# Expert weights in a two-layer transformer kernel: three chunks of each next expert go through spare memory and a GpSimd copy

## The chip, the cores and the metric

The kernel runs on one core of one Trainium2 chip, as one launch. The metric is the device time of one execution in microseconds (us): the median of several runs. Lower is better.

## What is computed

The reference is a first block (modulated attention, then a mixture of experts) followed by a second one of two layers (retention with sparse attention, then a gated recurrence, each with a dense feed-forward part), all in float32 on 256 tokens of width 1024. The part around the change is the mixture of experts of the first block:

```
N_EXPERTS = 32; TOP_K = 4; D_FF_EXPERT = D_MODEL = 1024
...
h2 = rms_norm(x, g_pre_ffn[l]) * (1.0 + sc2) + sh2
f = moe_ffn(h2, w_router[l], b_router[l], w1[l], b1[l], w2[l], b2[l])
x = x + gt2 * rms_norm(f, g_post_ffn[l])
```

Each token goes to four of 32 experts. An expert is a 1024x2048 matrix w1 with a bias b1, a clipped gated activation, and a 1024x1024 matrix w2 with a bias b2; that is 12 MiB of float32 weights. The 32 experts together are 384 MiB, and every one is read in full from device memory.

## The kernel before, in words

All weights of the program pass through one **ring** of twelve places in SBUF (`ring0` to `ring11`), each of 128 partitions x 2048 float32, 1 MiB. A place holds one **chunk**. Chunk n goes to place n % 12. SyncE (SP) issues all weight transfers, in one fixed order, in the function `_(sp)` from line 476 on; before each it waits until the place's last reader on TensorE has finished. TensorE tells that with the semaphore `chunk_done`, and within the experts with `job_chunk`, raised once by every chunk read. A transfer that has landed raises `landed[place]` by 16, and TensorE waits for that before it reads (line 984, `chunk_here`).

**Experts.** An expert has twelve chunks: 0 to 7 are the eight row blocks of w1 (line 530), 8 to 11 the four double row blocks of w2. TensorE works in **jobs** of 64 token slots (`SLOTS`). A job (`expert`, line 1025) runs `first_matrix` (line 987: eight chunks, eight matmuls of 512 columns each), the bias (line 996), the scatter of the job before (line 974), the gather of tokens for a later job (line 958), the turn of the activations (line 1003), and `second_matrix` (line 1015: four chunks, eight matmuls each). An expert with more than 64 tokens has two jobs in a row, which read the same twelve chunks; for the last job of expert e the vector engine has put the count of chunks before it into the table `jobs`, and it tells with `ends_listed` that it has. There are 34 jobs for these inputs, so two experts have a second job.

SP's loop `expert_chunks` (lines 522 to 532) issues the twelve chunks of expert e + 1 in order, chunk j after `job_chunk >= last_job + j + 1`, that is, when the last job of expert e has read its chunk j. Expert 0's chunks come into the places that the projections of the first block leave.

**The activation.** In a job, VectorE clips the two halves (lines 2344 and 2345), multiplies them (line 2348), and multiplies by ScalarE's sigmoid (line 2350); then TensorE may turn the result (line 1003).

**GpSimd (POOL)** does little: it issues small transfers, among them the table `late` of 3516 columns (1.8 MB: decay, cosines, sines, masks of the second block) when the heads of the first attention are done (`mix_saved`, lines 597 and 598), and the 1 MiB `cmp_w1` after `ssq_ready` 2, that is after the experts (line 602). It also adds squares (line 609) and multiplies one block by the last gain (line 619, which raises `y_gained`). TensorE waits for `late_loaded` ahead of the second block's projections (line 1292), and VectorE waits for it at line 2407.

**Memory used before the experts and not in them:** the attention bias `alibi` in `early_sb`, and in the arena `nat_bias` and the attention scores (columns 6144 to 12288). `late_sb` lay at columns 9600 and up.

```
def expert_chunks(e, wait):
    for j in range(PER_EXPERT):
        wait(j)
...
expert_chunks(0, lambda j: slot_free(C_MOE + j))
sp.wait_ge(S.ends_listed, 1)
with sp.Fori(0, E_N - 1) as e:
    last_job = sp.value_load(...)
    expert_chunks(e + 1, lambda j: sp.wait_ge(S.job_chunk, last_job + (j + 1)))
```

Of the kernel before, what the change touches and what calls it, by code (L numbers as in the profile page):

```python
# [10 lines left out]
ALU = mybir.AluOpType  # L11
# [13 lines left out]
DIFF_HEADS = 4  # L25
UNITS = 8
# [7 lines left out]
E_N = 32  # L34
# [4 lines left out]
LISTED = 64  # L39
# [15 lines left out]
RING = 12  # L55
CHUNK = 2048
N_ADA_A, N_WIN, N_ADA_B, N_WOUT = 8, 12, 16, 4
PER_EXPERT = 12
FIRST_HOME = (6, 7, 0, 3)
C_ADA_A = 0  # L60
C_WIN = C_ADA_A + N_ADA_A
# [2 lines left out]
C_MOE = C_WOUT + N_WOUT  # L64
# [44 lines left out]
ADDED_NORMS = (2,)  # L109
# [149 lines left out]
cmp_pos cmp_hidden cmp_bias cmp_act cmp_out cmp_saved cmp_scores cmp_shift cmp_exp cmp_probs cmp_turned cmp_turn_saved  # L259
nsa_max nsa_probs nsa_weighted nsa_out nsa_closed  # L260
hg_level hg_scores hg_placed hg_out hg_saved hg_sq hg_ssq hg_root hg_gated
ffn_split ffn_part ffn_kept ffn_sum ffn_silu ffn_hidden y_gained y_total y_root y_scale y_out_saved y_out_also out_stored""".split()


class Chain:
# [14 lines left out]
def two_layer_program(nc, x, c, w_ada, b_ada, g_pre_mix, g_post_mix, w_in, w_out, lam_q1, lam_k1, lam_q2,  # L280
# [4 lines left out]
    with ExitStack() as ctx:  # L285
        def sbuf(name, cols, dt=F32, rows=P):
            return ctx.enter_context(nc.sbuf_tensor(name, [rows, cols], dt))

        S = namedtuple("Semaphores", NAMES)(*[ctx.enter_context(nc.semaphore(n)) for n in NAMES])
        landed = [ctx.enter_context(nc.semaphore(f"landed{i}")) for i in range(RING)]  # L290


        ring = [sbuf(f"ring{i}", CHUNK) for i in range(RING)]
# [3 lines left out]
        mixT = sbuf("mixT", KT * T)  # L297
# [3 lines left out]
        jobs = sbuf("jobs", 2 * LISTED + 2 + E_N, I32, rows=1)  # L301
# [10 lines left out]
        def const(name):  # L312
            return early_sb[:, EARLY[name][0]:EARLY[name][1]]

        ident, ones, before, slot_id, fold, window = (
            const(n) for n in ("ident", "ones", "before", "slot", "fold", "window"))
        eps6, eps5 = const("eps")[:, 0:1], const("eps")[:, 1:2]
        alibi = const("alibi").rearrange("p (h n) -> p h n", h=DIFF_HEADS)
        cols_a, cols_b = carve(P), carve(2)

        silu_c = carve(KT * 32).rearrange("p (k m) -> p k m", m=32)
# [13 lines left out]
        def region(at, cols):  # L335
            assert at + cols <= 15900
            return arena[:, at:at + cols]
# [52 lines left out]
        diag = sq[:, 1024:1280]  # L390
        wanted, rank_of, chosen, job_scratch = (region(8512 + ALL_JOBS * i, ALL_JOBS) for i in range(4))
        job_cols = region(9580, 4)

        late_sb = region(9600, N_LATE)
        assert 9600 + N_LATE <= 13312 + 256
# [63 lines left out]
        final_gain, sum_slots = hT[:, 0:1024], cmp_act  # L459
        y_sums, y_total, y_mean = sum_slots[:, 0:5], sum_slots[:, 8:10], sum_slots[:, 10:11]  # L460
        junk = [region(1536, 512), region(2048, 512)]

        def x_block(a, half):
            return x_rows[:, a, 512 * half:512 * half + 512]
# [13 lines left out]
        def _(sp):  # L478
            def slot_free(n):

                if n >= RING:
                    sp.wait_ge(S.chunk_done, n - RING + 1)

# [37 lines left out]
            w1_view = w1[0].rearrange("e (k p) n -> e k p n", p=P)  # L521
            w2_view = w2[0].rearrange("e (c p k) n -> e c p k n", p=P, k=2)

            def expert_chunks(e, wait):
                for j in range(PER_EXPERT):
                    wait(j)
                    home = ring[(C_MOE + j) % RING]
                    if j < 8:
                        src = w1_view[bass.ds(e, 1), j].rearrange("a p n -> p (a n)")
                    else:  # L530
                        src = w2_view[bass.ds(e, 1), j - 8].rearrange("a p k n -> p (a k n)")
                    sp.dma_start(home[:, :], src).then_inc(landed[(C_MOE + j) % RING], 16)  # L532

            expert_chunks(0, lambda j: slot_free(C_MOE + j))
            sp.wait_ge(S.ends_listed, 1)
            with sp.Fori(0, E_N - 1) as e:
                last_job = sp.value_load(jobs[0:1, bass.ds(e + (2 * LISTED + 2), 1)], min_val=0, max_val=PER_EXPERT * 48)
                expert_chunks(e + 1, lambda j: sp.wait_ge(S.job_chunk, last_job + (j + 1)))

            sp.wait_ge(S.count_ready, 1)  # L540
            last_job = sp.value_load(jobs[0:1, 2 * LISTED + 1:2 * LISTED + 2], min_val=0, max_val=PER_EXPERT * 48)
# [30 lines left out]
        def _(pool):  # L572
# [21 lines left out]

            pool.wait_ge(S.mix_saved, DIFF_HEADS)
            pool.dma_start(h_tok, x[0].rearrange("(a p) d -> p a d", p=P)).then_inc(S.tok_loaded, 16)
            pool.wait_ge(S.mix_saved, UNITS)
            pool.dma_start(late_sb, late).then_inc(S.late_loaded, 16)

            pool.wait_ge(S.ssq_ready, 2)  # L600
            for i, v in enumerate((cmp_w1_k_2, cmp_w1_v_2)):
                pool.dma_start(cmp_w1_sb[:, i, :, :], v[0].rearrange("(j p) n -> p j n", p=P)).then_inc(S.cmp_loaded, 16)

# [12 lines left out]
            pool.dma_start(final_gain, bass.AP(final_norm_g_2.tensor, 0, [[0, P], [1, D]])).then_inc(S.late_loaded, 16)  # L616
            pool.wait_ge(S.late_loaded, 32)
            pool.wait_ge(S.sq_ready, down_squares_at(1, 3))
            nc.gpsimd.tensor_tensor(x_block(0, 0), x_block(0, 0), final_gain[:, 0:512], ALU.mult).then_inc(S.y_gained, 1)

        N_VEC = 9 + 4

# [2 lines left out]
        def _(pe):  # L625
# [663 lines left out]
                    pe.wait_ge(S.turned_saved, UNITS + (RET_SSQ_AT[p] - NSA_FIRST) // NSA_STEP)  # L1289
                nc.tensor.matmul(bank[RET_SSQ_BANK[p]][:, :], ones, ret_sq, start=True, stop=True).then_inc(S.ret_ssq, 1)  # L1290

            pe.wait_ge(S.late_loaded, 16)
            for slot in range(EIN_SLOTS):
                even_half(slot // 2, slot % 2)
                u, odd = divmod(slot - NSA_FIRST, NSA_STEP)
# [294 lines left out]
        def _(act):  # L1590
# [25 lines left out]
            at = KT  # L1616
            for v in (b_ada, g_pre_mix, g_post_mix, g_pre_ffn, g_post_ffn, norm_mix_g_2, norm_ffn_g_2):
                n = v.shape[0] * v.shape[1] // P
# [49 lines left out]
            for slot in range(WIN_SLOTS + WIN_TAIL):  # L1668
                if slot < WIN_SLOTS and slot % 2:
                    i = slot // 2  # L1670
# [309 lines left out]
            def down_norm(layer):  # L1980
# [32 lines left out]
                if layer == 0:  # L2013
                    scaled(1, 0, x_block(0, 0), y_block(0, 0))
                    gain_mixed(0)
                else:
                    act.wait_ge(S.y_gained, 1)
                    scaled(1, 0, x_block(0, 0), x_block(0, 0))

            def gain_mixed(a):  # L2020
# [804 lines left out]
```

## Time and profile before

| | |
|---|---|
| median of 3 runs | 1952.63 us (1951.38 to 1952.81) |
| the profiled execution | 1953.24 us, its span 1951.2 us |
| TensorE matmul busy | 1888.3 us (97% of the span) |
| TensorE weight load busy | 1140.7 us (58%) |
| VectorE, ScalarE, GpSimd busy | 666.0, 368.4, 33.9 us |
| granted TensorE clock | 1.00 over the whole span |
| read from device memory | 562.49 MB, 289 GB/s over the span |
| chain that ended last | TensorE 80%, transfers 13%, SP's queue 4% |

The span runs from the first to the last instruction; the execution's time is 2.0 us longer. Times in the rows further on are from the span's start. The experts are the stretch from about 200 to 1177 us, half of the span. Busy time of TensorE is modelled for pipelined matmuls, so a high share doesn't tell by itself that TensorE sets the time there: the chain of waits does.

### The profile page before, as it was taken

To read this page: it belongs to the slowest core of one execution; us is meant where nothing else is said; L and a number is where in the kernel's file an instruction comes from. 1 tells how busy PE (TensorE), PEld (TensorE's weight loads), DVE (VectorE), ACT (ScalarE), POOL (GpSimd) and SP (SyncE) were. 2 spreads that over 40 slices of the span, in tenths; PEclk is the share of its full clock that TensorE was granted. 3 is DMA by queue.
4 is the path that set the end of the run, shared out by engine and by line. 5 is a ranking of instruction groups with operands and counts; after the bars stand their busy time and mean duration, and the time that the engine had idled before them with its cause. 6 is when DMAs were issued, how large, how long until landed. Compare 5 with 4: busy or idle time off the path is not lost.

```text
span 1951.2 us, 25656 instructions
## 1 busy us (share of the span) xinstructions
PE 1888.3 (97%) x9793; PEld 1140.7 (58%) x9794; DVE 666.0 (34%) x1263; ACT 368.4 (19%) x803; POOL 33.9 (2%) x54
## 2 busy tenths in 40 slices
PE   8999999999999999999999989999999999999998
PEld 6877544333334434443333337878887589888864
DVE  2451411111111111111110113454666557555564
ACT  2232211110111111110110113442111121221111
POOL 2200000000000000000000001000000000000000
PEclk9999999999999999999999999999999999999999
DMA  9959699999989979999999999323545453345430
GB/s 365 276 227 410 265 392 421 422 422 422 422 341 393 422 305 422 422 422 422 422 422 422 422 419 317 108 90 126 173 173 173 130 172 108 101 136 164 163 118 22
DMA packets 156462, 564.46 MB, mean 289 GB/s; under 512 B 10766, under 2 KB 93992, under 8 KB 101872
## 3 DMA queue, kind: packets, MB, share of 16 engines
q1 hardware_dynamic: 153312, 554.96, 73.4%
q0 software_dynamic: 2336, 7.87, 1.3%
q8 instruction: 45, 0.74, 0.2%
q10 hardware_dynamic: 752, 0.75, 0.1%
q14 instruction: 17, 0.14, 0.0%
HBM read 562.49 MB, written 1.05 MB: 289 GB/s over the span
## 4 chain that ended last, share of the span: by engine, by line
PE 80%; DMA 13%; SPq 4%; DVE 1%; issue 1%; ACT 1%; ACTq 0%; DVEq 0%
PE psum L987 16%; DMA ring<-in_w_dram 12%; PE psum L1364 12%; PE psum L1015 9%; PE psum L1456 6%; PE psum L1508 6%; PE psum L1156 5%; SPq L532 4%; PE psum L743 3%; PE psum L810 3%; PE psum L958 3%; PE psum L974 2%; PE psum L1392 2%; PE psum L1531 1%; PE psum L996 1%; PE psum L1454 1%
## 5 line engine op out<-in xcount | busy, mean ns | idle before, releaser
L987 PE MATMUL psum<-ring,arena 128*64 128x512 f32 x2176 | 491.0, 596 | 39.0 <-DMA ring<-in_w_dram 39.0
L987 PEld LDWEIGHTS psum<-ring,arena 128*64 128x64 f32 x2176 | 151.9, 137 | 370.3 <-issue 252.1
L2344 DVE TENSOR_SCALAR arena<-psum 128x512 f32<-128x512 f32 x34 | 23.5, 691 | 727.9 <-PE psum L996 727.9
L1015 PE MATMUL psum<-ring,arena 128*64 128x512 f32 x1088 | 241.2, 595 | 3.9 <-ACT arena L1730 0.7
L1015 PEld LDWEIGHTS psum<-ring,arena 128*64 128x64 f32 x1088 | 77.5, 137 | 145.0 <-issue 144.1
L1726 ACT ACTIVATE arena<-arena 128x512 f32<-128x512 f32 x34 | 21.4, 630 | 547.9 <-DVE arena L2344 547.9
L1364 PE MATMUL psum<-arena,mixT 128*128 128x256 f32 x528 | 120.9, 379 | 0.0
L1364 PEld LDWEIGHTS psum<-arena,mixT 128*128 128x128 f32 x528 | 98.8, 190 | 12.6
L1508 PE MATMUL psum<-hT,ring 128*128 128x256 f32 x384 | 86.0, 379 | 0.0
L1364 PE MATMUL psum<-ring,hT 128*128 128x256 f32 x352 | 83.5, 379 | 0.0
L1508 PEld LDWEIGHTS psum<-hT,ring 128*128 128x128 f32 x384 | 71.9, 190 | 10.9 <-issue 1.9
L958 PE MATMUL psum<-arena 128*128 128x128 f32 x544 | 75.1, 281 | 0.0
L958 PEld LDWEIGHTS psum<-arena 128*128 128x128 f32 x544 | 65.9, 191 | 11.7 <-issue 11.7
L1364 PEld LDWEIGHTS psum<-ring,hT 128*128 128x128 f32 x352 | 66.6, 190 | 8.9
L974 PEld LDWEIGHTS psum<-arena 64*128 64x128 f32 x544 | 49.8, 186 | 32.9 <-issue 28.4
L974 PE MATMUL psum<-arena 64*128 64x256 f32 x544 | 67.9, 389 | 0.8 <-ACT arena L1734 0.8
L1156 PE MATMUL psum<-hT,ring 128*128 128x256 f32 x288 | 65.9, 382 | 0.0
L1156 PEld LDWEIGHTS psum<-hT,ring 128*128 128x128 f32 x288 | 53.5, 190 | 9.2 <-issue 2.4
L1716 ACT ACTIVATE arena<-psum,small 128x128 f32<-128x128 f32 x136 | 51.2, 456 | 7.3 <-PE psum L1090 5.0
L1734 ACT ACTIVATE arena<-psum 128x512 f32<-128x512 f32 x34 | 20.3, 597 | 170.7 <-PE psum L1015 170.7
L1456 PE MATMUL psum<-arena,sq 128*128 128x512 f32 x112 | 51.0, 592 | 0.0
L810 PE MATMUL psum<-hT,ring 128*128 128x256 f32 x192 | 43.8, 382 | 0.0
(486 smaller groups left out, 2205.9 us busy)
## 6 DMA issues: line engine op xcount, KB each, us to landing
ring<-in_w_dram SPq DMA_DIRECT2D x384, 1024.0 KB, 23.2
ring<-in_ffn_w_dram SPq DMA_DIRECT2D x66, 1024.0 KB, 5.3
ring<-in_w_ada_dram SPq DMA_DIRECT2D x16, 1024.0 KB, 11.5
ring<-in_odd_w_in_dram SPq DMA_DIRECT2D x16, 1024.0 KB, 5.6
ring<-in_even_w_in_dram SPq DMA_DIRECT2D x13, 1024.0 KB, 12.7
ring<-in_w_in_dram SPq DMA_DIRECT2D x12, 1024.0 KB, 37.0
ring<-in_ada_blocks_dram SPq DMA_DIRECT2D x8, 1024.0 KB, 17.4
ring<-in_w_out_dram SPq DMA_DIRECT2D x4, 1024.0 KB, 14.7
```

The lines of the kernel that those rows point to most:

```text
L532: sp.dma_start(home[:, :], src).then_inc(landed[(C_MOE + j) % RING], 16)
L743: mm = nc.tensor.matmul(home[:, at:at + n_out], lhs, rhs, start=(k == 0), stop=(k == KT - 1))
L810: mm = nc.tensor.matmul(home, lhs, rhs, start=(k == 0), stop=(k == KT - 1))
L958: nc.tensor.matmul(home[:, (k % 4) * P:(k % 4 + 1) * P], h_tok[:, a, k * P:(k + 1) * P], pick[:, a, :], start=(a == 0), stop=(a == TT - 1))
L974: mm = nc.tensor.matmul(bank[k // 2][:, (k % 2) * T:(k % 2 + 1) * T], y_sb[half, t * P:(t + 1) * P], st_sb[r][half, :], start=False, stop= ...
L987: mm = nc.tensor.matmul(bank[4 + q][64 * h:64 * h + 64, :], xg[:, k, SLOTS * r:SLOTS * (r + 1)], ring[(C_MOE + k) % RING][:, (2 * h + q) * ...
L1015: mm = nc.tensor.matmul(bank[7][64 * h:64 * h + 64, :], act_T[:, at:at + 64], w[:, k, 512 * h:512 * h + 512], start=(f == 0), stop=(f == 7))
L1156: mm = nc.tensor.matmul(home[:, at:at + n_out], lhs, rhs, start=(k == 0), stop=(k == KT - 1))
L1364: mm = nc.tensor.matmul(home, x[:, k, :], w[:, k, :], start=(first and k == 0), stop=(k == 3), skip_group_check=True)
L1456: return nc.tensor.matmul(bank[DOWN_PRODUCTS.index(name)], lhs, rhs, start=(c == 0), stop=(c == FFN_STEPS - 1))
L1508: mm = nc.tensor.matmul(home, lhs, rhs, start=(k == 0), stop=(k == KT - 1))
L1716: ins = nc.scalar.activation(dst[:, k, :], home[:, k * P:(k + 1) * P], ACT.Identity, bias=mod[:, 24 + 4 * r + k:25 + 4 * r + k], scale=pre ...
```

## The change

The first three chunks of the next expert (`STAGED = 3`) don't go to the ring. SP sends them to three spare places ("stage"): one in `early_sb` over `alibi`, one in the arena at 9600, one in two halves of 1024 columns (arena at 11648, and the upper half of `mixT`). GpSimd waits until such a chunk has landed (`staged[i]`) and until the last job of the expert before has read chunk i of the ring, runs a one-column subtraction, copies the chunk into the ring place, and raises `landed` of this place by 16 as a transfer would. SP's order becomes: chunks 3 to 11 of expert e + 1 into the ring, as before, then chunks 0 to 2 of expert e + 2 into the stage, each after the copy of chunk i of expert e + 1 out of it. Expert 1's three are issued right after expert 0's twelve.

Because the stage lies over the place of the table `late`, its load moves behind the experts (`pass_over`), ahead of `cmp_w1`, which also waits for `pass_over` now in place of `ssq_ready`. TensorE's own wait for `late_loaded` goes. The semaphore `y_gained` goes too; `squares_added` takes its part.

```
+STAGED = 3
+        stage = [[alibi_sb[:, 0:CHUNK]], [region(9600, CHUNK)], [region(11648, CHUNK // 2), mixT[:, CHUNK // 2:CHUNK]]]
...
-            def expert_chunks(e, wait):
-                for j in range(PER_EXPERT):
+            def expert_chunk(e, j):
+                if j < 8:
+                    return w1_view[bass.ds(e, 1), j].rearrange("a p n -> p (a n)")
+                return w2_view[bass.ds(e, 1), j - 8].rearrange("a p k n -> p (a k n)")
+
+            def ring_chunks(e, some, wait):
+                for j in some:
                     wait(j)
...
+                    sp.dma_start(ring[(C_MOE + j) % RING][:, :], expert_chunk(e, j)).then_inc(landed[(C_MOE + j) % RING], 16)
+
+            def stage_chunks(e, wait):
+                for i, parts in enumerate(stage):
+                    wait(i)
+                    cols = CHUNK // len(parts)
+                    for n, home in enumerate(parts):
+                        sp.dma_start(home, expert_chunk(e, i)[:, n * cols:(n + 1) * cols]).then_inc(staged[i], 16)
+
+            def first_stage_free(i):
+                if i == 0:
+                    sp.wait_ge(S.neg_max, UNITS)
+                    sp.wait_ge(S.turned, UNITS)
+                    sp.wait_ge(S.heads_out, UNITS)
+                if i == 2:
+                    sp.wait_ge(S.chunk_done, C_MOE)
+
+            def staged_copied(e, i):
+                at = (C_MOE + i) % RING
+                sp.wait_ge(landed[at], e * 16 + 16 * ((C_MOE + i) // RING + 1))
...
+            ring_chunks(0, range(PER_EXPERT), lambda j: slot_free(C_MOE + j))
+            stage_chunks(1, first_stage_free)
             sp.wait_ge(S.ends_listed, 1)
-            with sp.Fori(0, E_N - 1) as e:
...
+            with sp.Fori(0, E_N - 2) as e:
+                last_job = last_job_of(e)
+                ring_chunks(e + 1, range(STAGED, PER_EXPERT), lambda j: sp.wait_ge(S.job_chunk, last_job + (j + 1)))
+                stage_chunks(e + 2, lambda i: staged_copied(e + 1, i))
+            last_job = last_job_of(E_N - 2)
+            ring_chunks(E_N - 1, range(STAGED, PER_EXPERT), lambda j: sp.wait_ge(S.job_chunk, last_job + (j + 1)))
...
-            pool.wait_ge(S.mix_saved, UNITS)
+            pool.wait_ge(S.ends_listed, 1)
+            with pool.Fori(0, E_N - 1) as e:
+                last_job = pool.value_load(jobs[0:1, bass.ds(e + (2 * LISTED + 2), 1)], min_val=0, max_val=PER_EXPERT * 48)
+                for i, parts in enumerate(stage):
+                    at, cols = (C_MOE + i) % RING, CHUNK // len(parts)
+                    pool.wait_ge(staged[i], e * (16 * len(parts)) + 16 * len(parts))
+                    pool.wait_ge(S.job_chunk, last_job + (i + 1))
+                    nc.gpsimd.tensor_tensor(region(15700 + i, 1), ones[:, 0:1], ones[:, 0:1], ALU.subtract)
+                    for n, home in enumerate(parts):
+                        ins = nc.gpsimd.tensor_copy(ring[at][:, n * cols:(n + 1) * cols], home)
+                    ins.then_inc(landed[at], 16)
+
+            pool.wait_ge(S.pass_over, 1)
             pool.dma_start(late_sb, late).then_inc(S.late_loaded, 16)
-
-            pool.wait_ge(S.ssq_ready, 2)
...
-            nc.gpsimd.tensor_tensor(x_block(0, 0), x_block(0, 0), final_gain[:, 0:512], ALU.mult).then_inc(S.y_gained, 1)
+            nc.gpsimd.tensor_tensor(x_block(0, 0), x_block(0, 0), final_gain[:, 0:512], ALU.mult).then_inc(S.squares_added, 1)
...
-            pe.wait_ge(S.late_loaded, 16)
...
-                    act.wait_ge(S.y_gained, 1)
+                    act.wait_ge(S.squares_added, 2 * len(ADDED_NORMS) + 1)
```

## Rows read from the trace of the kernel before

**Rows 1.** Stretches of the span: engines' busy us, clock, DMA share, GB/s.

```profile
200.00:575.00 375.00, 357.72 (x1884) 148.26 (x1884) 67.10 (x149) 54.21 (x122) 0.00 (x0) 1.00 0.97 402
577.00:877.00 300.00, 298.83 (x1602) 126.19 (x1602) 46.87 (x91) 45.08 (x100) 0.00 (x0) 1.00 0.93 387
877.00:1170.00 293.00, 268.31 (x1391) 104.17 (x1388) 40.25 (x74) 36.54 (x80) 0.00 (x0) 1.00 1.01 421
1170.00:1215.00 45.00, 42.42 (x217) 30.80 (x215) 17.27 (x29) 16.85 (x37) 5.38 (x4) 1.00 1.07 325
```

**Rows 2.** The chain that ended last: start us, us, what.

```profile
243.15 13.88 PE psum L987 x64
262.80 7.09 PE psum L1015 x32
...
717.59 13.73 PE psum L987 x64
737.07 7.09 PE psum L1015 x32
...
1075.10 26.98 DMA ring<-in_w_dram
...
1135.12 27.00 DMA ring<-in_w_dram
```

**Rows 3.** TensorE's timeline in one job of the transfer-bound stretch: start, us.

```profile
554.76 7.22 PE L987 MATMUL psum<-ring,arena 128*64 128x512 f32 x32
562.53 1.94 PE L987 MATMUL psum<-ring,arena 128*64 128x512 f32 x8 [0.56 <-DMA ring<-in_w_dram]
...
569.98 1.94 PE L987 MATMUL psum<-ring,arena 128*64 128x512 f32 x8 [0.55 <-DMA ring<-in_w_dram]
```

**Rows 4.** Two pauses of the transfers, columns as in rows 1.

```profile
195.00:205.00 10.00, 9.11 (x48) 5.58 (x50) 8.12 (x35) 4.23 (x12) 0.00 (x0) 1.00 0.09 36
...
710.00:720.00 10.00, 9.90 (x49) 3.50 (x49) 1.68 (x6) 3.27 (x8) 0.00 (x0) 1.00 0.00 0
```

**Rows 5.** Line 532's issues in five windows: count, durations, first and last start.

```profile
L532 SPq DMA_DIRECT2D ring<-in_w_dram x4: 333/333/333, 228.2 to 237.7; - x4
...
DMA to landing us min/median/max: 4.9/5.6/6.8
...
L532 SPq DMA_DIRECT2D ring<-in_w_dram x8: 332/333/337, 245.2 to 257.2; - x8
...
L532 SPq DMA_DIRECT2D ring<-in_w_dram x3: 333/333/333, 264.9 to 268.3; - x3
...
DMA to landing us min/median/max: 7.7/8.4/9.2
...
L532 SPq DMA_DIRECT2D ring<-in_w_dram x8: 332/333/336, 719.5 to 731.5; - x8
...
L532 SPq DMA_DIRECT2D ring<-in_w_dram x4: 332/332/333, 739.2 to 744.3; - x4
...
DMA to landing us min/median/max: 6.0/7.1/8.3
```

**Rows 6.** GpSimd's arithmetic, by line and shape.

```profile
L609 POOL TENSOR_TENSOR sq<-sq 128x512 f32<-128x512 f32 x2 | 3.1, 1528 | 4.2 <-ACT sq L1593 4.1 <-POOL sq L609 0.2
L619 POOL TENSOR_TENSOR xT<-xT,hT 128x512 f32<-128x512 f32 x1 | 1.3, 1262 | 65.6 <-ACT arena L1991 65.6
```

**Rows 7.** VectorE's timeline in the job that follows the second pause.

```profile
733.80 0.69 DVE L2348 SCALAR_TENSOR_TENSOR arena<-arena 128x512 f32<-128x512 f32 x1
734.53 1.07 DVE L2350 TENSOR_TENSOR arena<-arena 128x512 f32<-128x512 f32 x1
```

**Rows 8.** The table `late`: its transfer (KB, us to landing), VectorE before and at its use.

```profile
arena<-in_late_dram POOLq DMA_DIRECT2D x1, 1758.0 KB, 11.7
...
1203.23 0.18 DVE L2406 COPY arena<-small 128x32 f32<-128x32 f32 x1
...
L2415 DVE SCALAR_TENSOR_TENSOR early_sb<-psum,arena x4: 957/958/959, 1225.5 to 1256.1; 128x768 f32<-128x768 f32 x4
```

More of the change, by code:

```diff
@@ L261 @@
 hg_level hg_scores hg_placed hg_out hg_saved hg_sq hg_ssq hg_root hg_gated
-ffn_split ffn_part ffn_kept ffn_sum ffn_silu ffn_hidden y_gained y_total y_root y_scale y_out_saved y_out_also out_stored""".split()
+ffn_split ffn_part ffn_kept ffn_sum ffn_silu ffn_hidden y_total y_root y_scale y_out_saved y_out_also out_stored""".split()
 class Chain:
@@ L289, in two_layer_program @@
         S = namedtuple("Semaphores", NAMES)(*[ctx.enter_context(nc.semaphore(n)) for n in NAMES])
+        staged = [ctx.enter_context(nc.semaphore(f"staged{i}")) for i in range(STAGED)]
         landed = [ctx.enter_context(nc.semaphore(f"landed{i}")) for i in range(RING)]
@@ L317, in two_layer_program @@
         eps6, eps5 = const("eps")[:, 0:1], const("eps")[:, 1:2]
-        alibi = const("alibi").rearrange("p (h n) -> p h n", h=DIFF_HEADS)
+        alibi_sb = const("alibi")
+        alibi = alibi_sb.rearrange("p (h n) -> p h n", h=DIFF_HEADS)
         cols_a, cols_b = carve(P), carve(2)
@@ L522, in _ @@
             w2_view = w2[0].rearrange("e (c p k) n -> e c p k n", p=P, k=2)
-            def expert_chunks(e, wait):
-                for j in range(PER_EXPERT):
-                    wait(j)
[L527 to L532, printed above, removed]
@@ L534, in _ @@
-            expert_chunks(0, lambda j: slot_free(C_MOE + j))
-            sp.wait_ge(S.ends_listed, 1)
-            with sp.Fori(0, E_N - 1) as e:
-                last_job = sp.value_load(jobs[0:1, bass.ds(e + (2 * LISTED + 2), 1)], min_val=0, max_val=PER_EXPERT * 48)
-                expert_chunks(e + 1, lambda j: sp.wait_ge(S.job_chunk, last_job + (j + 1)))
+            def expert_chunk(e, j):
+                if j < 8:
+                    return w1_view[bass.ds(e, 1), j].rearrange("a p n -> p (a n)")
+                return w2_view[bass.ds(e, 1), j - 8].rearrange("a p k n -> p (a k n)")
@@ new lines, in first_stage_free, with last_job_of @@
+            def first_stage_free(i):
[8 more added lines that the diff above has]
+                sp.wait_ge(landed[at], e * 16 + 16 * ((C_MOE + i) // RING + 1))
+            def last_job_of(e):
+                return sp.value_load(jobs[0:1, bass.ds(e + (2 * LISTED + 2), 1)], min_val=0, max_val=PER_EXPERT * 48)
```

## The prediction

> **What bounds the kernel now.** I read first the stretches, then the chain of waits, then both sides of the points where the chain changes hands. In the stretches [rows 1] TensorE and the transfers are both nearly full while the experts run: TensorE 299 of 300 us from 577 to 877, the transfers at share 1.01 and 421 GB/s from 877 to 1170. The chain [rows 2] says who is late. Before 577 and from 877 on it runs over the ring's transfers, at the end two experts in 1135.12 - 1075.10 = 60.0 us; between them it is TensorE alone. In the transfer-bound stretch [rows 3] TensorE starts w1's chunks 0 to 3 in one go at 554.76 and then waits about 0.55 us for each of chunks 4 to 7, which arrive 2.48 us apart, the last at 569.98; from there the job runs without a wait. So what sets a job's time there is the landing of chunk 7.
>
> The transfers pause in spite of this [rows 4]: about 195 to 205, in the router, and 710 to 720; a third of the same kind, near 580, lies where TensorE becomes the bound. The two later ones are the experts with two jobs: no place comes free in the first. After 710 to 720 the transfers never pause again until the experts end, so the end of the experts is the end of that pause plus what is then left to fetch. Time can be won only before that, or there.
>
> **What the stage brings.** The reading on sight is three chunks, 3 x 2.48 = 7.4 us, at each pause that counts. I follow SP's order instead.
>
> Second pause: SP resumes at 719.5 [rows 5], when chunk 0 has been read (717.59 + 13.73 / 8 = 719.3 [rows 2]). With the stage, chunks 0 to 2 have come in the pause, but the next in SP's order is chunk 3, which waits for the fourth read, 717.59 + 4 x 1.72 = 724.5. Of 7.4 us, 5.2 are given back: 2.3 left. Then chunk 8 waits for the reader of chunk 8, in the second matrix: 737.07 + 7.09 / 4 = 738.8 [rows 2], and it is in fact issued at 739.2 already now [rows 5]. So its issue does not move at all. All that is won is that the queue ahead of it is emptier: it now lands 6.0 us after its issue (the least of its window), and where the queue was almost empty it was 4.9 to 6.8 [rows 5]. Bounds: 0 to 1.1 us; I take 0.4, nearer to 0, since chunks 3 to 7, issued from 724.8 at 2.48 each, still end only about 740.
>
> First pause: the same place decides. Chunks 0 to 2 of expert 1 come during the router, but its chunk 8 goes on waiting for job 0's. Chunks 0 to 2 of expert 2 are issued some 7 us earlier than now, right after the last of expert 1 at 237.7 and not at 245.2 [rows 5]; chunk 3 then waits for 243.15 + 4 x 1.735 = 250.1, and chunk 8 for 262.80 + 1.77 = 264.6 [rows 2], issued at 264.9 now [rows 5]. It lands 7.7 us after that, against 4.9 to 6.8 with little queued: 0.9 to 2.8 us if the queue were empty, 0 if other traffic takes it back; I take 0.8, because chunk 7 would be in the queue still.
> The pause near 580 wins nothing: TensorE is the bound behind it.
> Sum: -0.8 reaches the second pause through TensorE's chain, -0.4 is added there: **-1.2 us**. Both survive only up to the end of the experts, where transfers bind.
>
> **What the copies cost.** GpSimd now stands between landing and reader in all 31 later experts. Where TensorE binds, the copy starts when a place comes free, at 719.3, and its reader is the next job, from 737.07 + 7.09 = 744.2 [rows 2]: three copies have 25 us, hidden. Where transfers bind it starts at the landing. Counting back from 569.98 [rows 3], chunk 0 landed at 569.98 - 7 x 2.483 = 552.6. TensorE is back in step at chunk 7 if chunk 2 is in the ring by 569.98 - 5 x 1.72 = 561.4. The three copies run one after another, so they are free as long as 3C <= 561.4 - 552.6 = 8.8 us, **C <= 2.9 us**, C being wait, one-column operation and copy. Beyond, TensorE is late by 3C - 8.8; this isn't summed over experts, as the next one starts again from its own landings, but it counts twice: once before the second pause, once at the last expert.
>
> No row has a GpSimd copy. The nearest are its two-input operations of 512 columns, 1.26 and 1.53 us [rows 6], which read 1024 values a lane. If reading costs, a copy of 2048 is twice that: 2.5 to 3.1 us. Upper end: as much per column written, 4 x 1.53 = 6.1 us. Lower end: VectorE's 0.69 us for 512 columns [rows 7] is 2.8 four times, and 2.1 if a third of the 0.69 doesn't grow with the columns. I take 2.5 plus 0.2 for the rest, C = 2.7, by the row of 1.26, as the other stands beside VectorE's work: no cost.
> The Trainium skill (GPSIMD Engine Reference, Performance versus the Vector engine and Engine selection) says the two-input rate is the floor of one shared read port and that one-input operations run roughly at line rate; with its 1.2 GHz that is an estimate of 1.7 us for 2048 columns, which would leave the sum as it is and make the slow copy less likely. No row here shows it.
>
> **Other edits.** `late` moves from the stretch ahead of the router to the end of the experts, about 1180. Its 1758 KB [rows 8] are 1.8 MB / 421 GB/s = 4.3 us of transfer, freed where nobody on the chain waits for a transfer (the router's vector work is the chain there): 0. Behind the experts it competes with the second block's first chunks; transfers are full there [rows 1], but none is on the chain. It took 11.7 us to land; from 1180 that is 1192, VectorE comes to its wait at 1203.4 and uses the table from 1225.5 [rows 8]: covered by 11 us. If that cover were gone, at most 4.3 us. `cmp_w1` goes out within microseconds of before. On GpSimd the added squares queue behind three short issues, which are over when the squares come: 0. TensorE's removed wait was for a table long there: 0. The semaphore exchange: 0. SP issues one more transfer per expert (0.33 us [rows 5]), with tens of us in hand.
>
> **Sum.** Against the execution of 1953.2 us (span 1951.2 and 2.0 around it): 1952.0. It lies 0.6 above the median, so **1951.4 us** as a median.
>
> **Rivals.**
> 1. **Slow copies.** C above 3.8 us makes it slower by more than can be told: 2 x (3C - 8.8) - 1.2. At C = 4.7, between the rows' 3.1 and 6.1, that is +9.4, 1962 us; at 6.3 it is +19, 1972. The place is w1's chunks 0 to 2 in the transfer-bound jobs, and the sign turns at C = 3.1. For it speaks that GpSimd is twice as slow as VectorE on the same shape [rows 6, 7]; against, that a copy reads one stream only.
> 2. **The stage counts in full.** If chunk 8's reader is not what holds the queue, because places come free earlier than I read, each of two pauses wins 2.3 us (1948) up to 7.4 us (1938). For: it adds a quarter to the memory. Against: the issues at 264.9 and 739.2 already follow the reads of chunk 8 by 0.3 us.
> 3. **The copies hold VectorE.** If a copy blocks VectorE's operations with two inputs from SBUF at lines 2348 and 2350, the turn behind them, which TensorE reaches at about the same time, is late by up to one copy, 2.5 us. In the TensorE-bound jobs the copies run from 1.7 to about 10 us after the job's start at 717.59, line 2348 starts at 733.80, 16.2 after it [rows 7]: they meet only if C is over 4.8. Then six jobs before the second pause could lose 6 x 2.5 = 15 us: 1966. The Trainium skill (SBUF, Who interferes with whom) states this lock: a two-input operation contends with a GpSimd one that reads SBUF, and the loser fully blocks. By this rule and my C nothing meets, and it takes off nothing.
> 4. **The moved table is late.** +4.3 us: 1956.
>
> **How the numbers follow.** Forecast 0.70, slow copies 0.16, full stage 0.07, held VectorE 0.03, late table 0.04. A measurement of this kernel tells about 0.2% from no change, 3.9 us. Faster by more: the full stage and a little of the forecast's edge, 0.08. Slower by more: slow copies, the lock, and half of the late table, 0.20 with a rest for what I don't see. Same: 0.72. The forecast's own range is 1948.5 to 1955. For 8 in 10 the range is 1948 (the small form of the full stage) to 1959.5 (slow copies up to C = 4.3); left out are the larger form, the slower half of the slow copies, and the lock.
>
> **What would show it.** In the changed profile: SP's issues of line 532 or its successor for chunk 8 still at about 264 and 738; the pauses at 710 to 720 about 5 us longer on the ring but with 3 MB moved in them, and a second short gap before 739; GpSimd busy 31 x 3 x 2.5 = 230 us; waits of TensorE at w1's chunks 0 to 2 on GpSimd of under 1 us each where transfers bind; the last expert's jobs ending within 2 us of 1177. A copy row over 3.8 us, chunk 8 issued earlier, or waits of the turn at line 1003 for VectorE prove the forecast wrong.

## The result and the profile after

The change makes the kernel slower. Nine runs give a median of 1968.94 us (1959.73 to 1972.53), nine of the kernel before on the same chip 1954.53 us (1951.38 to 1958.97): a ratio of **1.0066, 95% interval 1.0052 to 1.0079**. By this ratio that is 12.9 us; the two medians lie 14.4 us apart. The forecast was 1951.4 us in a range of 1948.0 to 1959.5. The profiled execution took 1965.09 us, its span is 1963.2, 12.0 more than before's 1951.2.

First the stretches of the changed kernel, with the columns of [rows 1]; the last two lines answer to [rows 1] at a finer cut.

```profile
577.00:877.00 300.00, 287.50 (x1512) 120.12 (x1510) 61.56 (x84) 41.57 (x92) 56.89 (x63) 0.98 0.92 375
877.00:1170.00 293.00, 275.74 (x1432) 113.05 (x1430) 60.87 (x80) 38.60 (x85) 63.92 (x70) 0.98 1.01 420
...
640.00:700.00 60.00, 55.34 (x282) 22.64 (x280) 14.61 (x16) 7.72 (x17) 12.42 (x14) 0.94 1.01 421
663.00:672.00 9.00, 9.00 (x39) 2.94 (x40) 1.68 (x6) 2.89 (x7) 0.11 (x1) 0.87 1.01 422
```

Two things are new. VectorE is busy for 61.56 us from 577 to 877 with 84 instructions, where it had 46.87 us with 91, and TensorE, full before, has holes of 12.5 us there and no longer its full clock. GpSimd, idle here before, is busy for 231.1 us over the whole span, where it was for 33.9.

The chain of waits says where it ends last. The second matrix's start marks a job. Before, these starts lie 26.57 us apart where TensorE binds. Two lines of TensorE's timeline of the kernel before, five jobs apart:

```profile
577.67 7.09 PE L1015 MATMUL psum<-ring,arena 128*64 128x512 f32 x32
710.51 7.09 PE L1015 MATMUL psum<-ring,arena 128*64 128x512 f32 x32
```

After, in the chain (line 1056 is the second matrix, 1028 the first, 2388 and 2390 VectorE's two products, lines 2348 and 2350 before):

```profile
580.04 7.09 PE psum L1056 x32
...
633.18 7.09 PE psum L1056 x32
640.27 13.73 PE psum L1028 x64
...
656.48 1.95 DVE arena L2388
658.44 0.02 issue
658.46 2.78 DVE arena L2390
...
663.13 8.12 PE psum L1056 x32
...
692.65 8.75 PE psum L1056 x32
...
720.88 7.09 PE psum L1056 x32
...
1181.82 7.11 PE psum L1056 x32
```

The three jobs from 633.18 to 720.88 take 29.95, 29.52 and 28.23 us in place of 26.57, together 8.0 us. VectorE stands in the chain there, where before the chain from 577 to 877 ran over TensorE alone, and the second matrix behind it takes 8.12 and 8.75 us for 7.09.

The lines themselves: durations in ns (least, median, most), and who waited for line 2390.

```profile
L2388 DVE SCALAR_TENSOR_TENSOR arena<-arena x34: 691/693/2381, 221.7 to 1178.5; 128x512 f32<-128x512 f32 x34
L2390 DVE TENSOR_TENSOR arena<-arena x34: 1051/1076/2787, 223.3 to 1179.3; 128x512 f32<-128x512 f32 x34
...
who waited for it (us, times):
  PEld psum L1044: 36.3, 18
  PE psum L1044: 32.3, 17
```

The same instruction on a block of the same size takes 0.69 us or up to 2.38, and 1.07 or up to 2.79. Line 1044 is the turn, 1003 before; there TensorE waits for VectorE 17 times, for 32.3 us in all, where before it did so once, for 0.8 us. In 17 of the 34 jobs a product is longer than undisturbed. The timelines of GpSimd and VectorE in two jobs that follow each other show when:

```profile
625.11 1.89 POOL L637 COPY ring<-early_sb 128x2048 f32<-128x2048 f32 x1
627.53 1.89 POOL L637 COPY ring<-arena 128x2048 f32<-128x2048 f32 x1
631.58 1.03 POOL L637 COPY ring<-arena 128x1024 f32<-128x1024 f32 x1
...
655.99 1.89 POOL L637 COPY ring<-early_sb 128x2048 f32<-128x2048 f32 x1
658.43 1.89 POOL L637 COPY ring<-arena 128x2048 f32<-128x2048 f32 x1
661.10 1.03 POOL L637 COPY ring<-arena 128x1024 f32<-128x1024 f32 x1
```

```profile
629.91 0.69 DVE L2388 SCALAR_TENSOR_TENSOR arena<-arena 128x512 f32<-128x512 f32 x1
630.64 1.07 DVE L2390 TENSOR_TENSOR arena<-arena 128x512 f32<-128x512 f32 x1
...
656.48 1.94 DVE L2388 SCALAR_TENSOR_TENSOR arena<-arena 128x512 f32<-128x512 f32 x1
658.46 2.77 DVE L2390 TENSOR_TENSOR arena<-arena 128x512 f32<-128x512 f32 x1
```

In the first job both products start after the second copy has ended (629.42) and before the third starts (631.58), and they keep their times. In the second one each meets a copy and ends 0.5 to 0.9 us after it: 656.48 + 1.94 = 658.42, the copy 655.99 + 1.89 = 657.88; 658.46 + 2.77 = 661.23, the copy 658.43 + 1.89 = 660.32. It goes the other way too: copies that met a product already running took up to 2.37 us for 1.89, and up to 1.75 for 1.03. And TensorE, from its timeline:

```profile
661.28 0.66 PE L1044 MATMUL psum<-early_sb,arena 128*128 128x128 f32 x4 [2.80 <-DVE arena L2390]
```

Last, what started the copies: GpSimd's waits (engine, line, waited for: us in total, times, longest).

```profile
POOL arena L635 <- DMA early_sb<-in_w_dram: 588.1, 25, 30.2
POOL arena L635 <- PE psum L1028: 205.2, 6, 105.1
```

At 25 of 31 experts the first copy waited for its transfer and only at 6 for its place.

The collisions also keep themselves up. A held job takes about 29.9 us, as long as an expert's transfers, so the next copies come at the same point of the next job: the first one starts 6.9, 6.7 and 6.7 us ahead of the second matrix in the jobs that reach it at 321, 351 and 381 us. In kernel 5 (the numbers of kernels are those of the experiments below), where the same copies hold nothing, they move on in each job and lie over a product in 6 jobs, not in 17.

**Where the 12.0 us of the span come from.** Comparing the second matrix's start of each job: +3.0 us in the job that starts at 243, where the clock fell (below); +12.2 at the sixth job (381.26 for 369.07); then transfers bind, the copies cost nothing there, and the lateness melts to +1.6 (489.77 for 488.18) and stands at +2.4 at 580.04. The three jobs above add 8.0: +10.4 at 720.88, where the transfers start again after the second pause. The next ten held jobs bring it to +23.8 at most (893.72 for 869.92), which melts when transfers bind again, and the experts end at +12.0 (1181.82 for 1169.85). Behind them nothing is added. So 12.0 is 2.4 + 8.0 + 1.6, and of the many collisions only those count that stand just ahead of the second pause. Only the 8.0 is shown to come from the collisions. The 2.4 is about what the clock's fall leaves by itself: kernel 2 has the same fall at 242 us and no held product, and stands at +2.0 at the same job. The 1.6 has no known cause; kernels 1, 2 and 5, none with a held product, show 1.0 to 1.8 over the same stretch.

### The profile page after: what moved, and what is told of

It is laid out like the page before. It is cut to its first block, busy times and chain, and to the rows that moved or that the text cites. A ratio compares the mean times of both kernels' runs of the same rounds, so it can differ in the third digit from the quotient of the medians.

```text
span 1963.2 us, 26277 instructions
## 1 busy us (share of the span) xinstructions
PE 1894.4 (96%) x9793; PEld 1149.2 (59%) x9794; DVE 720.7 (37%) x1263; ACT 368.0 (19%) x803; POOL 231.1 (12%) x272
## 4 chain that ended last, share of the span: by engine, by line
PE 83%; DMA 7%; DVE 6%; SPq 2%; issue 1%; ACT 1%; POOL 0%; POOLq 0%; DVEq 0%; ACTq 0%
PE psum L1028 20%; PE psum L1404 12%; PE psum L1056 11%; PE psum L1496 6%; PE psum L1548 6%; PE psum L1197 5%; DMA ring<-in_w_dram 4%; PE psum L784 3%; PE psum L851 3%; DVE arena L2390 2%; PE psum L1432 2%; PE psum L999 2%; PE psum L1037 2%; PE psum L1571 1%; DMA arena<-in_w_dram 1%; DMA mixT<-in_w_dram 1%
## 5 line engine op out<-in xcount | busy, mean ns | idle before, releaser
L1028 PEld LDWEIGHTS psum<-ring,arena 128*64 128x64 f32 x2176 | 156.6, 137 | 330.8 <-issue 289.1
L1056 PEld LDWEIGHTS psum<-ring,arena 128*64 128x64 f32 x1088 | 79.6, 142 | 153.2 <-issue 152.3
L635 POOL TENSOR_TENSOR arena<-early_sb 128x1 f32<-128x1 f32 x93 | 21.3, 229 | 866.6 <-DMA early_sb<-in_w_dram 588.1
L637 POOL COPY ring<-arena 128x2048 f32<-128x2048 f32 (+1 forms) x62 | 90.7, 1463 | 0.0
L1548 PE MATMUL psum<-hT,ring 128*128 128x256 f32 x384 | 86.0, 379 | 0.0
L1548 PEld LDWEIGHTS psum<-hT,ring 128*128 128x128 f32 x384 | 71.9, 190 | 10.9 <-issue 1.9
L1197 PE MATMUL psum<-hT,ring 128*128 128x256 f32 x288 | 65.9, 382 | 0.0
L2390 DVE TENSOR_TENSOR arena<-arena 128x512 f32<-128x512 f32 x34 | 61.4, 1807 | 2.1 <-ACT arena L1766 0.9
L637 POOL COPY ring<-early_sb 128x2048 f32<-128x2048 f32 x31 | 59.5, 1920 | 0.0
```

Source lines behind the costliest of these rows:

```text
L637: ins = nc.gpsimd.tensor_copy(ring[at][:, n * cols:(n + 1) * cols], home)
L1028: mm = nc.tensor.matmul(bank[4 + q][64 * h:64 * h + 64, :], xg[:, k, SLOTS * r:SLOTS * (r + 1)], ring[(C_MOE + k) % RING][:, (2 * h + q) * ...
L1056: mm = nc.tensor.matmul(bank[7][64 * h:64 * h + 64, :], act_T[:, at:at + 64], w[:, k, 512 * h:512 * h + 512], start=(f == 0), stop=(f == 7))
L1197: mm = nc.tensor.matmul(home[:, at:at + n_out], lhs, rhs, start=(k == 0), stop=(k == KT - 1))
L1548: mm = nc.tensor.matmul(home, lhs, rhs, start=(k == 0), stop=(k == KT - 1))
L2390: V.tensor_tensor(act_pairs, hidden_pairs[0], hidden_pairs[1], ALU.mult).then_inc(S.act_ready, 1)
```

## The experiments

The theory from the profile: a GpSimd copy that reads SBUF holds those operations of VectorE that read two operands from SBUF until it is done; what decides is where in the job the copies fall. The rivals: the copies' length by themselves, GpSimd's writes or the new order of transfers, and something else at that place of the job.

**1. The same copies, kept away from the activation.**

```
-                    pool.wait_ge(S.job_chunk, last_job + (i + 1))
+                    pool.wait_ge(S.job_chunk, last_job + 9)
```

> The changed kernel lost 12.0 us by the end of the experts. Theory L (held VectorE): GpSimd's copies, when they fall on VectorE's two-input operations of the activation, hold these, the turn of the activation comes late and TensorE idles. Here each copy also waits for the ninth read (chunk 8) of the last job of the expert before, which lies behind the activation of that job; in the transfer-bound jobs it has passed before the chunk lands. L expects lines 2388 and 2390 back at 0.69 and 1.07 us in every job, no idle time of TensorE at line 1044, and a total near the kernel before: 0.9995 to 1.001 of it, up to 3 us more in an execution where the clock falls in the first jobs. Theory W (TensorE waits for chunks that stand in the copy) expects no gain or a loss against the changed kernel, since the copies come later: 1.007 or more. Theory S (SP's new order of transfers is late) expects no change: 1.006.

Measured: 1954.30 us, ratio **1.0002 [0.9993, 1.0011]**; the whole loss is gone. In its trace the two products have one duration in all 34 jobs:

```profile
L2388 DVE SCALAR_TENSOR_TENSOR arena<-arena x34: 692/692/694, 221.9 to 1166.6; 128x512 f32<-128x512 f32 x34
L2390 DVE TENSOR_TENSOR arena<-arena x34: 1066/1074/1081, 223.5 to 1167.4; 128x512 f32<-128x512 f32 x34
```

What costs is when the copies run, and not how much they copy.

**2. A write of the same length without a read.** GpSimd writes zeros in place of the copy, at the same places and with the same waits; chunks 0 to 2 of w1 are thus zero for experts 1 to 31.

```
-                        ins = nc.gpsimd.tensor_copy(ring[at][:, n * cols:(n + 1) * cols], home)
+                        ins = nc.gpsimd.memset(ring[at][:, n * cols:(n + 1) * cols], 0.0)
```

> The copies of the changed kernel are replaced by GpSimd memsets of the same ring places, with the same waits and the same raising of landed, so chunks 0 to 2 of all experts but the first are zero weights. A memset writes SBUF and reads none. If it is the reading that holds VectorE (the rule of the Trainium skill, SBUF, Who interferes with whom), lines 2388 and 2390 run at 0.69 and 1.07 us though GpSimd works at the same places, and the total is 0.999 to 1.001 of the kernel before. If any GpSimd work holds VectorE, both lines still reach 1.9 us and more where they meet it, and the total is above 1.003. Theory S expects 1.006.

Measured: 1954.74 us, ratio **1.0002 [0.9992, 1.0011]**. A job of its GpSimd timeline, and VectorE's in the same job:

```profile
654.94 1.80 POOL L637 MEMSET ring<- 128x2048 f32 x1
```

```profile
656.07 0.69 DVE L2388 SCALAR_TENSOR_TENSOR arena<-arena 128x512 f32<-128x512 f32 x1
656.80 1.07 DVE L2390 TENSOR_TENSOR arena<-arena 128x512 f32<-128x512 f32 x1
```

This write of 1.80 us lies over the first product as the copies did, and holds nothing. A write lies over a product in seven jobs of this trace, and the products take 0.69 and at most 1.09 us in all 34. So it is the copy's read that holds them.

**3 and 4. Copies in the kernel before.** No stage, no change of any transfer: three copies of the dead `alibi` onto itself an expert, from the read of chunk 7 (which puts them on the activation) or of chunk 8 (behind it).

```
+                    if i == 0:
+                        pool.wait_ge(S.job_chunk, last_job + 8)   # or + 9
...
+                    nc.gpsimd.tensor_copy(alibi_sb, alibi_sb).then_inc(S.probe, 1)
```

> The kernel before, without any stage: GpSimd copies the dead attention bias onto itself three times (128x2048 each, about 6 us) in the last job of each expert but the last, starting when that job has read its chunk 7, so that the copies run from 0.2 to 6.5 us behind the first matrix and meet lines 2348 and 2350. No weight waits for them and SP's order is the old one. L expects line 2350 to end 2 to 3.5 us late in each such job; this is on the end's chain in the first two jobs and in the four that lie in the TensorE-bound stretch before the second pause: 6 x 2 to 6 x 3.5 = +12 to +21 us, 1.006 to 1.011. W, S and a late table expect 1.000.

> The same three copies in the kernel before, one read later: they start when the last job of each expert has read its chunk 8, about 2 us into the second matrix, when lines 2348 and 2350 are over. L expects 1.000 (0.999 to 1.001) and both lines at 0.69 and 1.07 us. If GpSimd's load on memory or on anything else in the job were the cost, it would stay: as much as with the copies one read earlier.

Measured: 2055.47 us, ratio **1.0524 [1.0507, 1.0540]**, and 1954.54 us, ratio **1.0002 [0.9992, 1.0012]**. One job of the first, by engine:

```profile
293.26 1.89 POOL L610 COPY early_sb<-early_sb 128x2048 f32<-128x2048 f32 x1
295.69 1.89 POOL L610 COPY early_sb<-early_sb 128x2048 f32<-128x2048 f32 x1
...
293.33 2.38 DVE L2359 SCALAR_TENSOR_TENSOR arena<-arena 128x512 f32<-128x512 f32 x1
295.74 2.75 DVE L2361 TENSOR_TENSOR arena<-arena 128x512 f32<-128x512 f32 x1
...
298.54 1.12 PE L1014 MATMUL psum<-early_sb,arena 128*128 128x128 f32 x4 [3.21 <-DVE arena L2361]
```

The mechanism stands without the stage: the same 93 copies cost 100 us on the activation, and nothing some 7 us later in the job (from 2.2 us after the second matrix's start on). The size was missed, 1.0524 for an expected 1.006 to 1.011: a job is late by 3.2 us of waiting and by a second matrix of 7.4 to 9.0 us in place of 7.09, more than the 3.3 us (29.83 - 26.57) that a job has in hand where transfers bind. So those jobs lost too, which the expectation had left out.

**5. The products with one operand in PSUM.** The unguarded change, but the clipped half and the first product stay in PSUM, so that each product reads one operand from SBUF.

```
-                V.tensor_scalar(lin, both[:, :, 1], LIMIT, ...)
+                V.tensor_scalar(both[:, :, 1], both[:, :, 1], LIMIT, ...)
-                chain.link(V.scalar_tensor_tensor(out=lin, in0=lin, scalar=1.0, in1=glu, ...))
+                chain.link(V.scalar_tensor_tensor(out=both[:, :, 1], in0=both[:, :, 1], scalar=1.0, in1=glu, ...))
-                V.tensor_tensor(act_pairs, hidden_pairs[0], hidden_pairs[1], ALU.mult)
+                V.tensor_tensor(act_pairs, lin_psum, hidden_pairs[1], ALU.mult)
```

> The changed kernel with its unguarded copies, but VectorE's two operations of the activation take one operand from PSUM: the clipped linear half stays in its PSUM banks, the first product is written there, and the second product reads it from there. Each of the two now has one input from SBUF. Theory L in the form 'two inputs from SBUF are what a GpSimd copy holds' expects both lines at their undisturbed time (0.7 and about 1.1 us, at most 0.2 more for PSUM) in every job, whatever the copies do beside them, and a total of 0.999 to 1.001 of the kernel before. If a GpSimd copy holds every VectorE operation, the two lines still reach 1.9 to 2.8 us in some ten jobs and the total stays above 1.004.

Measured: 1955.44 us, ratio **1.0000 [0.9991, 1.0008]**. The copies start by the same rule and lie over a product in 6 jobs, by 0.3 to 0.8 us, and no product is held:

```profile
L2389 DVE SCALAR_TENSOR_TENSOR psum<-psum,arena x34: 699/700/700, 225.1 to 1172.4; 128x512 f32<-128x512 f32 x34
L2391 DVE TENSOR_TENSOR arena<-psum,arena x34: 1055/1070/1097, 226.7 to 1173.1; 128x512 f32<-128x512 f32 x34
```

**6. Its control**, the same activation in the kernel before.

> The kernel before with the activation in PSUM alone (no stage, no GpSimd copy), the control for the two kernels that have it. Theory: without a GpSimd copy there is nothing for it to avoid, so the ratio is 1.000, between 0.9995 and 1.0005, and the lines of the two products keep about 0.69 and 1.07 us. Rival: the operations with an operand in PSUM are shorter or longer by themselves, and the TensorE-bound jobs move with them; then a part of the gain of the reordered kernel (0.9980) belongs to it: ratio 0.999 or less.

Measured: 1953.81 us, ratio **0.9996 [0.9988, 1.0005]**: worth nothing that can be told, as expected.

**7. Copies in pieces of 512 columns.**

```
+                        for c in range(0, cols, 512):
+                            ins = nc.gpsimd.tensor_copy(ring[at][:, n * cols + c:n * cols + c + 512], home[:, c:c + 512])
```

> The changed kernel, each copy cut into pieces of 512 columns (twelve instructions for the three chunks, an estimated 0.6 us each, three chunks in 7.5 us). L with a lock that is held for one instruction expects VectorE to be held for at most about 0.6 us by each of the two lines, where the changed kernel shows up to 1.7: line 2388 at most 1.3 us, line 2390 at most 1.7, TensorE about 1 us late in a job that meets copies and not 3, no fall of the clock there, and a total of 1.001 to 1.003. If the queue of GpSimd has to run empty before VectorE gets in, the cost stays as in the changed kernel or grows: 1.006 and more.

Measured: 1954.70 us, ratio **1.0006 [0.9996, 1.0017]**, no loss that can be told, and a little less than the expected 1.001 to 1.003. The products take at most 0.97 and 1.49 us:

```profile
L2389 DVE SCALAR_TENSOR_TENSOR arena<-arena x34: 691/693/973, 221.4 to 1167.8; 128x512 f32<-128x512 f32 x34
L2391 DVE TENSOR_TENSOR arena<-arena x34: 1061/1073/1485, 223.1 to 1168.5; 128x512 f32<-128x512 f32 x34
```

The products are longer by 0.28 and 0.41 us at most, less than one piece of 0.61 us. So a product is held by the instruction that it meets; it doesn't wait for all the copying that stands queued. Four pieces take 2.3 us for 2048 columns in place of 1.89, and the time doesn't show it.

**8. Copies twice as long**, kept behind the activation as in 1: fourteen one-column operations ahead of each, C = 4.0 us, 3C = 12.0.

> The guarded kernel (each copy waits for the ninth read) with 14 more one-column operations ahead of each copy, which at an estimated 0.14 us each make C, the time from landing to ready, about 4.0 us in place of 2.05. It tests the prediction's slack: copies are free up to 3C = 8.8 us, and cost 2 x (3C - 8.8) beyond, once ahead of the second pause and once at the last expert: +6.4 us at C = 4.0, 1.0033; in the trace +3.2 at the second pause, +6.4 at the end of the experts. If TensorE has other slack in the transfer-bound jobs the total stays within 1.001.

Measured: 2026.24 us, ratio **1.0361 [1.0344, 1.0378]**, eleven times the expected excess. TensorE's timeline in one job, and the waits of its weight loads for the copies in all (engine, line: us, times, longest):

```profile
554.54 10.52 PE L1030 MATMUL psum<-ring,arena 128*64 128x512 f32 x48 [2.21 <-POOL ring L639]
...
PEld psum L1030 <- POOL ring L639: 158.2, 72, 3.1
```

GpSimd starts 2.0 us into the second matrix, since this kernel has the guard, and the next job begins 5.1 us later: 12 us of copying can't be done before chunks 1 and 2 are wanted. So this run tests the slack behind a place that comes free, not the 8.8 us behind a landing, for which the prediction's formula was made. Whether that formula holds stays open. What the run does show: a job with such copies takes about 30.6 us, longer than the transfers' 29.83, and then it is paid in every job, and not twice in all, as the prediction had it.

**9. A version that beats both kernels.** This is kernel 5, but SP issues the next but one expert's chunk 0 to the stage ahead of chunks 8 to 11 of the ring, and not behind them.

```
-                ring_chunks(e + 1, range(STAGED, PER_EXPERT), ...)
-                stage_chunks(e + 2, lambda i: staged_copied(e + 1, i))
+                ring_chunks(e + 1, range(STAGED, 8), ...)
+                stage_chunks(e + 2, lambda i: staged_copied(e + 1, i), (0,))
+                ring_chunks(e + 1, range(8, PER_EXPERT), ...)
+                stage_chunks(e + 2, lambda i: staged_copied(e + 1, i), (1, 2))
```

> The kernel of the run with the activation in PSUM, and SP's order changed: the stage transfer of chunk 0 of expert e + 2 goes ahead of chunks 8 to 11 of expert e + 1, and not behind them. The prediction held that chunk 8's place paces the transfers behind each pause (issued at 264.9 and 739.2), which leaves a gap of about 2 us that one stage chunk fills. If so, the transfers are about 2 us further on at each of the two pauses that count, and the experts end 3 to 5 us earlier than with the activation in PSUM alone: 0.9975 to 0.999 of the kernel before. If something else paces them there, no gain: 1.000.

Measured: 1951.05 us, ratio **0.9980 [0.9972, 0.9989]**. It shared its runs with kernel 5, and the two intervals don't touch, so the order alone is worth about 0.2%. The transfers behind the second pause, of kernel 1 and then of this one (the eighth number is their share):

```profile
725.00:730.00 5.00, 5.00 (x26) 1.64 (x22) 0.00 (x0) 0.00 (x0) 0.00 (x0) 1.00 0.86 360
735.00:740.00 5.00, 4.90 (x28) 2.22 (x28) 0.60 (x2) 2.38 (x6) 1.81 (x2) 1.00 0.67 254
```

```profile
725.00:730.00 5.00, 5.00 (x28) 1.55 (x26) 0.18 (x1) 0.00 (x0) 0.00 (x0) 1.00 1.00 387
735.00:740.00 5.00, 5.00 (x26) 1.76 (x24) 0.00 (x0) 1.22 (x4) 0.00 (x0) 1.00 1.00 416
```

With the change's order the transfers stand still a second time (share 0.00 from 738 to 739 in kernel 1), as chunk 8 waits for its reader; a chunk that has a place of its own fills that gap. Chunk 8 is issued 2.11 us after the second matrix's start both in the kernel before (739.18 for 737.07) and in kernel 1 (738.27 for 736.16): the stage doesn't move it.

**10. The late table alone**, in the kernel before.

> The kernel before with one edit of the change alone: the table late and cmp_w1 are loaded behind the experts, and TensorE's wait for the table is gone; no stage, no copy. Theory (as in the prediction): ratio 1.000, and VectorE's first use of the table is covered by about 11 us. Rival: the early transfer of the table takes 4.3 us from the weights in front of the router, or the late one delays the second block: a ratio off 1 by 0.001 to 0.002, and VectorE waiting at the table's first use.

Measured: 1955.40 us, ratio **1.0003 [0.9994, 1.0013]**. Its table lands 9.5 us after the issue, and TensorE is as late behind the experts as at their end (2.8 us, both).

## Why the prediction was wrong

**The step that failed** is the placing of the copies in time: "Where TensorE binds, the copy starts when a place comes free, at 719.3", and from it, in the rival of the held VectorE, "the copies run from 1.7 to about 10 us after the job's start", so that "they meet only if C is over 4.8". In the job at 640.27 they run from 655.99 to 663.12, 15.7 to 22.9 us after its start, right over the activation, which starts 16.2 us after it, as in [rows 7]. They meet with C at 2.1, well under 4.8, since at 25 of 31 experts the landing starts them. The prediction had what it needed for this: it says itself that after 720 "the transfers never pause again", and an expert takes 29.83 us to fetch while a job takes 26.57. Transfers are full although TensorE binds, so a landing comes some 3.3 us later in each next undisturbed job and moves over its phases, until it meets the activation; there, as shown above, it stays for up to ten jobs. A fixed phase was read from the one job that follows a pause, the one place where the place was late and the transfer early.

**The rival had the right mechanism and nearly the right price.** Its 15 us (six jobs of 2.5) stand against 12.9 measured; in the trace three jobs before the second pause lost 8.0, 5.3 in waiting and 2.7 in a slower second matrix, and the other 4.0 of its 12.0 are mostly clock and drift. That the two totals are near is partly luck: seven jobs were held ahead of the second pause, not six, and five of them cost nothing, as transfers bound behind them. Its chance of 0.03 was what the wrong phase left. The Trainium skill (SBUF, Who interferes with whom) says that a VectorE instruction with two SBUF inputs contends with a GpSimd one that reads SBUF, and not with one that only writes. The trace and the runs agree in each part: 0.69 and 1.07 us became up to 2.38 and 2.79 under a copy, stayed under a write (2), and stayed with one operand in PSUM (5). I weighed this rule and let a number of mine silence it.

**The other steps.**
- *What bounds.* Right. What stands at the second pause reached the end: +10.4 there, +12.0 at the end of the experts, +12.0 in the span. The lateness of up to 12.2 and 23.8 us elsewhere melted where transfers bind.
- *The stage, -1.2 us.* The reason is shown, the number isn't. Chunk 8's place holds the queue: without collisions the stage alone gives 1.0002, 1.0002 and 1.0000 (kernels 1, 2, 5), and filling the gap ahead of chunk 8 gives 0.9980. But 1.2 us are under what a ratio can tell here, and single executions scatter by more: the second pause comes 0.9 us earlier in kernel 1, and 2.2 us earlier in kernel 6, which has no stage. The rival "the stage counts in full" falls.
- *What the copies cost.* C is 0.13 of the one-column operation plus 1.89 or 2 x 1.0, about 2.05 us, against 2.7: below the bound of 2.9. The copy itself, 1.89 us, is nearer to the estimate of 1.7 us by the Trainium skill (GPSIMD Engine Reference, Engine selection) than to the 2.5 taken. Right that they are free at the ring: with them and without a collision the ratio is 1.000. That the cost "isn't summed over experts" is wrong once a job is longer than the transfers (8). The rival "slow copies" falls.
- *The other edits and the moved table, 0.* Right (10): the changed kernel is 12.0 us late at the experts' end and 12.0 in the span.
- *The signs foretold.* "Waits of the turn at line 1003 for VectorE" were to prove the forecast wrong, and they did. Chunk 8's issue and the second short gap came as foretold (9). GpSimd's 230 us were met by luck: of the 231.1 measured, 33.9 were there before, and the copies with their one-column operations added 197.

What stays open: the changed kernel's runs lie 12.9 us above, and the profiled execution lost 3.0 us in the first job by a fall of the clock. The timed runs have a mean granted clock of 0.987 to 0.994, but not where it fell, so I can't say how many had that. Nor is a drift of about 1 us explained that several kernels show when transfers begin to bind near 880, kernel 10 without a stage among them.

## What to carry to other kernels

Before a helper engine gets work beside a critical one, ask what starts it in the steady state. Where two rates differ (29.83 us of transfers, 26.57 of a job) whatever follows the one moves through the phases of the other, and "they don't meet" must hold for all of them. Where a meeting slows the faster side down to the rate of the slower one, the two stay together. A GpSimd copy that reads SBUF held VectorE's work on two SBUF operands for up to about its own length (1.7 us by a copy of 1.89, 0.4 by one of 0.61). Put it behind that work with one semaphore, cut it to pieces, or keep one operand in PSUM; with each of the three no loss that can be told was left here. And spare buffers help only where the transfer that the queue waits for gets one, or something is put ahead of it.

## What was not expected of the hardware

A GpSimd copy in float32 took 1.89 us for 128x2048, 1.04 for 1024 and 0.61 for 512 columns, which is 0.83 ns a column and 0.2 us besides, where its two-input operations took 1.26 us for 512 columns [rows 6]. A write alone was hardly shorter, 1.80 us.

Short waits of TensorE were often followed by a lower clock. Before, with waits of 0.55 us [rows 3], the granted clock was 1.00 all over the experts. After the wait of 2.80 us that ends at 661.28 it is 0.50 from 661.9 to 665.3, the level of 1.2 GHz, and back at 2.4 GHz behind that (so 0.87 on average from 663 to 672); the second matrix takes 8.12 us for 7.09. TensorE has twelve waits over 1.5 us in the experts of the changed kernel. The clock fell at seven of them (1.76 to 3.23 us) and not at the other five (1.53 to 1.83 us). In kernel 3 it fell in nearly every job, and the second matrix took up to 9.0 us. So a wait of 3 us cost up to 5.

In the first job, at 242 us, the clock fell to one half with no wait of TensorE over 0.3 us in the 6 us before it, and what made it fall isn't known:

```profile
242.00:249.00 7.00, 7.00 (x18) 2.28 (x18) 0.00 (x1) 1.50 (x4) 1.91 (x2) 0.51 0.99 394
```

That is the level of 1.2 GHz; the first matrix took 16.63 us in place of 13.88. From 236 to 250 the clock was below 1.00 in five of the twelve profiled executions, two of them of kernels without a stage (4 and 10: 0.88), and full in the kernel before, in 1 and in 7. So such a fall doesn't need the change. In 76 timed executions of the kernel before the mean granted clock is 0.995 to 1.000; those at 1.000 took 1951.3 to 1953.4 us, those at 0.995 and 0.996 1957.2 to 1960.2.
